# Where the loads of a group's gates and hidden values are issued in the V stage

## The reference, cut to what matters

```python
best, pos = lax.top_k(cand.reshape(tp, PEER_HEADS, PEER_TOPK * PEER_TOPK), PEER_TOPK)
ids = jnp.take_along_axis(cid.reshape(tp, PEER_HEADS, PEER_TOPK * PEER_TOPK), pos, axis=-1)
gates = jax.nn.softmax(best, axis=-1)
...
def block(args):
    xb, idb, gb = args
    h = jax.nn.gelu(jnp.einsum('td,thkd->thk', xb, u_table[idb]), approximate=False)
    w = (gb * h).astype(xb.dtype)
    return jnp.einsum('thk,thkd->td', w, v_table[idb]).astype(xb.dtype)
...
x = layer_norm(ALPHA * x + peer(x, peer_w_query, peer_sub_keys, peer_u, peer_v), ln2_g, ln2_b)
```

## Time and profile before

| what | value |
|---|---|
| median of 3 runs | 4085.16 us (4085.02 to 4093.54) |
| the profiled execution's own time | 4094.46 us |
| its span | 4092.7 us |
| mean granted TensorE clock of the span | 0.968 |
| PE busy / DVE busy / ACT busy / POOL busy | 96% / 64% / 26% / 36% |
| U stage ends, V stage's first matmul starts | 2845.6 us, 2853.4 us |
| last matmul of the V stage ends | 4049.4 us |

### The profile page before, as it was taken

The page is one execution under the profiler, slowest core; times in us unless marked ns, Lnnn a source line. Parts: engine busy times, 40 slices in busy tenths (PEclk is TensorE's granted clock), DMA queues, the critical chain, the costliest instruction groups (busy, mean ns, idle before and its releaser), DMA issues.

```text
span 4092.7 us, 70828 instructions
## 1 busy us (share of the span) xinstructions
PE 3908.7 (96%) x27864; PEld 3831.7 (94%) x27864; DVE 2617.1 (64%) x4474; ACT 1051.8 (26%) x914; POOL 1470.2 (36%) x497
## 2 busy tenths in 40 slices
PE   8999998796999999999999999999999999999996
PEld 7999998796999999999999999999999999999995
DVE  5776957656899299999972000001587787887867
ACT  3222322323222233333332222222222221222213
POOL 3232332344333333333334333434444344442311
PEclk9988988898999999999999999999999999999998
DMA  3221221221235656666666666665677778778752
GB/s 136 79 72 59 81 65 72 80 82 52 82 123 166 199 192 211 218 224 210 225 213 200 198 194 199 198 199 192 234 266 293 294 287 313 265 286 311 279 208 85
DMA packets 416196, 751.55 MB, mean 184 GB/s; under 512 B 19600, under 2 KB 343632, under 8 KB 355296
## 3 DMA queue, kind: packets, MB, share of 16 engines
q1 hardware_dynamic: 351936, 543.27, 39.4%
q0 software_dynamic: 22528, 134.30, 8.2%
q10 hardware_dynamic: 41632, 72.67, 5.0%
HBM read 677.60 MB, written 206.78 MB: 216 GB/s over the span
## 4 chain that ended last, share of the span: by engine, by line
PE 76%; DVE 14%; DMA 4%; issue 2%; ACT 2%; POOL 1%; SPq 1%; ACTq 0%; DVEq 0%; POOLq 0%
PE ps L534 52%; PE ps L778 19%; DMA wraw<-in_v_t 4%; DVE yb L1305 2%; PE ps L745 2%; DVE wl L1506 2%; PE ps L656 1%; PE ps L611 1%; PE ps L658 1%; ACT wh L837 1%; SPq L362 1%; DVE acc L1500 1%; DVE y_sp L1519 1%; DVE yfb L1314 0%; POOL wl L464 0%
## 5 line engine op out<-in xcount | busy, mean ns | idle before, releaser
L464 POOL TENSOR_TENSOR wl<-wraw,wh 128x2048 fp32r<-128x2048 f32 x202 | 961.0, 4758 | 1753.3 <-ACT wh L837 1753.3
L534 PE MATMUL ps<-xh,wh 128*128 128x272 f32 x5888 | 1241.3, 292 | 50.8 <-POOL xl L483 22.0
L534 PE MATMUL ps<-xh,wl 128*128 128x272 f32 x5888 | 1228.6, 290 | 0.0
L534 PE MATMUL ps<-xl,wh 128*128 128x272 f32 x5888 | 1225.2, 290 | 0.0
L534 PEld LDWEIGHTS ps<-xh,wh 128*128 128x128 f32 x5888 | 935.2, 191 | 63.9 <-issue 52.7
L534 PEld LDWEIGHTS ps<-xl,wh 128*128 128x128 f32 x5888 | 936.1, 191 | 0.0
L534 PEld LDWEIGHTS ps<-xh,wl 128*128 128x128 f32 x5888 | 930.5, 191 | 0.0
L837 ACT ACTIVATE wh<-wraw 128x2048 fp32r<-128x2048 f32 x328 | 628.5, 1916 | 1145.5 <-PE ps L778 732.8
L778 PE MATMUL ps<-Wh,wh 128*128 128x416 f32 x2048 | 721.9, 352 | 29.3 <-DVE wl L1506 21.2
L778 PE MATMUL ps<-Wh,wl 128*128 128x416 f32 x2048 | 724.8, 354 | 0.0
L778 PE MATMUL ps<-Wl,wh 128*128 128x416 f32 x2048 | 717.4, 350 | 0.0
(11 more groups left out here) (235 smaller groups left out, 2906.4 us busy)
## 6 DMA issues: line engine op xcount, KB each, us to landing
wraw<-in_u_t SPq DMA_DIRECT2D x128, 1024.0 KB, 5.0
v_rows<-in_v_t SPq DMA_DIRECT2D x256, 512.0 KB, 6.9
wraw<-in_v_t SPq DMA_DIRECT2D x128, 1024.0 KB, 5.1
wraw<-in_w_in SPq DMA_DIRECT2D x40, 1024.0 KB, 5.0
h_scratch<-hb ACTq DMA_DIRECT2D x64, 416.0 KB, 3.9
g_scratch<-gst ACTq DMA_DIRECT2D x13, 2048.0 KB, 7.7
gt<-g_scratch SPq DMA_DIRECT2D x16, 1664.0 KB, 14.1
hg<-h_scratch SPq DMA_DIRECT2D x16, 1664.0 KB, 20.5
```

What stands on the lines that cost most here:

```text
L464: nc.gpsimd.tensor_tensor(wl[:, u], wraw[:, u], f(wh[:, u]), ALU.subtract).then_inc(wlo, 1)
L534: ins = mat(out[:, h], w[:, u, k], m[:, k, halves[h]], start=(begin and k == ks[0] and w is wh and m is ah), stop=(end and k == ks[-1] and ...
```

## The change

`group_in` moves from SP's stream to ACT's, with the waits that guard it. On ACT the loads of group 0 stand behind the whole U stage: behind the last gelu, the last high part and the last stores of h. Those of group g+1 stand in group g's first iteration (m = 0), behind the high part of tile 8g+2. ACT's loop over pairs of tiles becomes a loop over groups with its 8 tiles written out. SP's stream keeps the weight tiles alone. No transfer, no computation and no semaphore count is otherwise changed.

```diff
-            for v in range(2):
-                sp.wait_ge(g_st[v], 16 * (NGC // 2 + 1))
-            for v in range(2):
-                sp.wait_ge(h_st[v], 32 * (EG // 4))
-            group_in(0)
             v_first()
-            sp.wait_ge(w_s, EG)
-            for v in range(2):
-                sp.wait_ge(h_st[v], 32 * (NKEY // 4))
-            group_in(1)
             v_pairs(0, EG // 4, EG // 2)
-            with sp.Fori(1, NG - 1) as g:
-                v_pairs(g, 0, EG // 4)
-                sp.wait_ge(w_s, g * EG + EG)
-                group_in(g + 1)
-                v_pairs(g, EG // 4, EG // 2)
-            with sp.Fori(NG - 1, NG) as g:
+            with sp.Fori(1, NG) as g:
                 v_pairs(g, 0, EG // 2)
...
             with C.loop(U_C, {h_out: 4}) as i:
                 u_four(i + (U_A + U_B))
...
+            def group_in(g):
+                for dst, src, q in ((gt[:].rearrange("p c e t -> p c (e t)"), gsrc, g_in),
+                                    (hg[:].rearrange("p (n u) t -> p n (u t)", u=2), hsrc, h_in)):
+                    s = src[g] if isinstance(g, int) else src[bass.ds(g, 1)].rearrange("o p n q -> (o p) n q")
+                    a.dma_start(dst, s).then_inc(q, 16)
+
+            for v in range(2):
+                a.wait_ge(g_st[v], 16 * (NGC // 2 + 1))
+            for v in range(2):
+                a.wait_ge(h_st[v], 32 * (EG // 4))
+            group_in(0)
             for e in range(EG):
                 a.wait_ge(wp_s, e + 1)
                 go(Wh[0][:, e], wt[e % 2][:], ACT.Copy).then_inc(wh_s, 1)
-            with a.Fori(0, (NG - 1) * EG // 2) as i:
-                for u in range(2):
-                    hi(i * 2 + (A_V + u + 2), u, i * 4 + (A_V + 2 * u + 2))
+            for v in range(2):
+                a.wait_ge(h_st[v], 32 * (NKEY // 4))
+            with a.Fori(0, NG - 1) as g:
+                for m in range(EG):
+                    hi(g * EG + (A_V + m + 2), m % 2, g * KT + (A_V + 2 * m + 2))
+                    if m == 0:
+                        a.wait_ge(w_s, g * EG + EG)
+                        group_in(g + 1)
```

More of the change, by code:

```diff
@@ L408, in _ @@
                              v_src[bass.ds(g, 1), m, d].rearrange("o j e c -> (o j) e c"), rows_in)
-            gsrc = g_dram.rearrange("c j (g e) t -> g j c (e t)", e=EG)
-            hsrc = h_dense.rearrange("(g n) p u t -> g p n (u t)", n=EG // 2)
             vs = v_t.rearrange("(g n u) p k c -> g n u p k c", u=2, n=EG // 2)
[L413 to L417, removed]
             def v_first():
@@ L1107, in _ @@
                 u_four(i + (U_A + U_B))
+            gsrc = g_dram.rearrange("c j (g e) t -> g j c (e t)", e=EG)
+            hsrc = h_dense.rearrange("(g n) p u t -> g p n (u t)", n=EG // 2)
+            def group_in(g):
[8 more added lines that the diff above has]
+            group_in(0)
             for e in range(EG):
```

## The result

The changed kernel has a median of 4115.87 us (4103.46 to 4132.46, 7 runs) beside 4090.31 us (4085.02 to 4094.42, 7 runs) of the kernel before; ratio 1.0067, interval 1.0046 to 1.0088. Two more jobs gave 1.0102 (1.0079 to 1.0124) and 1.0096 (1.0072 to 1.0121) for the same kernel. The forecast was 4081 us, within 4068 to 4104. Its profiled execution took 4125.55 us, 31.1 us more than the one before.

What follows compares the result with a forecast made beforehand. The V stage was taken as bound by TensorE at 9.06 us a tile, with 21.2 us of waits to save. +13.8 - 21.2 - 4 + 7 = -4.4 us gave a median of 4081 us, range 4068 to 4104.

Steps and rivals of the forecast that it cites:

- The start (+13.8): V stage's start: group 0's loads, late on ACT's queue, delay TensorE's first matmul; loss 13.8 us, bounds 11 and 22.5.
- The tile itself goes at the same pace: First V tile after the longer starting wait: same pace and no further clock cost, so nothing added to 13.8 us.
- the sum: Whole kernel against the profiled execution: +13.8 - 21.2 - 4 + 7 = -4.4 us.
- Tiles overtake the group (-21.2): Groups 2 to 15: tile 8g+4 no longer stands behind the group loads, taking off up to 21.2 us of TensorE's waits.
- E: In each group g of the V stage, the end of tile 8g, from which landing and due times are counted.
- Rival C: V tiles do not overtake and land as late as now; only SP's long issues go: +5, 4090 us; chance 0.12.
- hg late (+7): Groups 2 to 15: hg lands late in busy groups, 5 of 14 waiting 1 to 1.5 us, plus a little clock: +7 us.
- The byte sum: Window before hg is complete: 9.65 MB in 24.7 us puts hg at E + 26 to 27, lighter groups E + 23 to 24.
- The clock (-4): Two low-clock stretches behind TensorE's waits go with those waits; 5.1 us of lost work, of which 4 taken as gain.
- ACT's issue hides: Group loads issued on ACT: about 1 us for hg, even 5 us hidden by ACT's idle time; cost nothing.
- the groups' part: Groups' terms together, waits for tiles -21.2, clock -4 and late hg +7: -18 us.

Runs made afterwards that it cites:

- paced: The changed kernel with GpSimd clearing a 128x1024 tile after each of the 32 gathers of h, to issue them further apart; ratio 1.0046 to the kernel before.
- pool_late: The changed kernel with GpSimd starting its 32 gathers of h only when TensorE has finished V tile 1; ratio 1.0047 to the kernel before.
- early_2: Repeat of the kernel with group 0's loads on SP and later groups' loads on ACT, groups 2 to 15 one tile earlier than the change; 4062.61 us, ratio 0.9938.
- third: The changed kernel unaltered, run once more for a third profile; ratio 1.0096 to the kernel before.
- sp_first: The changed kernel with group 0's loads back on SP ahead of the first V tiles, groups 1 to 15 staying on ACT; ratio 0.9998 to the kernel before.
- act_first: The kernel before with group 0's loads alone moved to ACT behind the U stage, all other groups on SP; ratio 1.0082 to the kernel before.
- sp_late: The kernel before with group 0's loads on SP but held back until the last gelu of the U stage; ratio 1.0031 to the kernel before.
- late_act: The kernel before, loads early on SP, with ten extra copies on ACT that DVE waits for before W of group 0; ratio 1.0081 to the kernel before.
- early: First job with group 0's loads on SP and later groups' on ACT, groups 2 to 15 one tile earlier than the change; 4061.37 us, ratio 0.9949.

## Why the prediction was wrong, step by step

**The start (+13.8): right in mechanism and size.** Measured 14.4 us; hg had landed when DVE started at 2866.0, for 2865.2 forecast. That the longer wait would cost no further clock was right too in `paced` and `pool_late`, where nothing else disturbs the stage's start.

**The step that failed: "The tile itself goes at the same pace".** I concluded it from the clock alone, from a wait of 18.6 us earlier in the kernel. GpSimd issued no gathers behind that one. In the changed kernel its gathers of h go out 1.25 us apart while TensorE stands idle, and a slow stretch follows, 24.1 us in the profiled pair, where the prediction had nothing. The kernels with the wait alone (`pool_late`, `paced`) are at 1.0047 and 1.0046 and the changed kernel at 1.0067, 1.0102 and 1.0096, so an estimate across jobs gives the stretch 0.2 to 0.6%, 8 to 23 us. No rival had it. Without it the sum would have been +14.4 - 7.7, 7 us of loss in the profiled pair, inside the range.

**Tiles overtake the group (-21.2): right for the tiles.** ACT's waits for V tiles fell from 185.1 to 90.7 us but did not go. In nine groups tile 8g+4 kept ACT waiting until E + 18 to 20, later than my E + 17, still ahead of the E + 22.8 at which it is due; some 7 us of each such wait are ACT's usual idle time. Rival C is out. That the 21.2 us of TensorE's waits go with it was wrong: the late hg took their place, as the next step says. The Trainium skill has it that transfers of the three queues interleave on the same 16 DMA engines and that issuing from several of them saves only the sequencer's issue time (Trainium Kernel Development and Optimization, Key Constraints). By the second half the tiles would have stayed as late as they were; here the measurement decides against that, 90.7 us for 185.1; with the first half, turns between the queues, it agrees.

**hg late (+7): too low.** DVE waited for hg in each group: 0.9 to 5.4 us in groups 2 to 14, 33.3 us in all. These waits ended at E + 24.5 to 28.9, 26.4 in the mean, where I had 23 to 27 for the landing; I had taken 5 of 14 groups to wait. One group, timeline of DVE, with E = 3267.3:

```profile
3288.43 2.28 DVE L1503 TENSOR_TENSOR wl<-wraw,wh 128x2048 fp32r<-128x2048 f32 x1
3292.74 1.09 DVE L1484 TENSOR_TENSOR wt<-hg,gt 128x416 f32<-128x416 f32 x2 [2.02 <-DMA hg<-h_scratch]
```

The byte sum was sound within 2 us for these groups, and 7.4 us of TensorE's waits come from them. The other 6.1 us is the last group's, which I had not set apart: hg took ACT's queue 12.85 us to issue there and reached DVE 10.1 us late. Timeline of ACT and its queue:

```profile
3930.43 12.85 ACTq L1094 DMA_DIRECT2D hg<-h_scratch  x1
3943.48 1.91 ACT L815 ACTIVATE wh<-wraw 128x2048 fp32r<-128x2048 f32 x1 [11.89 <-PE ps L756]
```

The kernel before has the same long issue in the same group, 11.10 us, and I had put it down to what stood ahead of it on SP's queue. ACT's queue had only gt ahead of it, as in every group. The last group's issue is long in each of the twelve profiles with its load at this place, 9.9 to 11.1 us on SP and 11.4 to 15.6 on ACT; with the same loads one tile earlier (`early_2`) it took 1.60 us, while three others took 6 to 11. What sets the length is open. New waits are 13.5 us instead of 7, and up to 27.7 in `third`.

**The clock (-4): nothing.** The profile after has two dips behind waits in the groups, as before (length, busy, clock, DMA share, GB/s), and so the lost work is the same:

```profile
3970.00:3978.00 8.00, 5.66 (x18) 0.57 0.57 216
4002.00:4009.00 7.00, 4.85 (x25) 0.76 0.26 82
```

0.43 x 8 + 0.24 x 7 = 5.1 us, the sum I had for the kernel before.

The first dip lies behind the last group's wait of 6.1 us. The second lies behind a wait of 2.1 us that the kernel before has too, without a dip behind it (`PE ps <- DVEq`, L798 here and L820 there).

**ACT's issue hides: right.** 0.7 to 5.4 us in 15 groups, behind it only the high part of tile 8g+3; the last delayed that part by 4.7 us, without a wait of TensorE of its own.

Together the groups' part was to be -18 us and was -7.7 us in the profiled pair, +10.5 in `third` against the same profile of before, and -0.8 us (-6.5 to +4.5) in the runs of `sp_first`. Why it differs so from run to run is open.

## What stays open

That an idle TensorE and unpaused gathers are both needed is shown: take away either and the stretch goes. That they are enough is not: `act_first`'s profile has both and hardly a pause. Whether the gathers' pace or their number before the first V matmul counts (11 and 12 with a slow stretch, 0 to 7 without, 12 beside a busy TensorE) was not tested. How gathers of 128 elements of 4 bytes hold TensorE up is not. The late release of ACT and DVE would fit a path for instructions or semaphore updates that both use, but no run separates the two. How long the wait must be is open as well: 17.3 us (`sp_late`) were too few, 20.6 us (`late_act`) enough, yet the two also differ in when the gathers begin.

## What to carry to other kernels

A load that opens a stage belongs in the stream that gets there first, for a queue's issue point is the place in its engine's instruction stream. When loads change queues, add up the bytes of the window and ask when the moved one lands, then move it until it lands with room: here one tile of 9 us turned no change (`sp_first`) into 0.5 to 0.6% faster. Before a gain in waits is believed, read it in a second profile: the same kernel had 13.5, 18.3 and 27.7 us of them. A wait that is only priced by its length may cost more behind it: look at what other engines do during it.

## What the runs showed of the hardware that was not expected

- The slow stretch: 20 matmuls of 416 columns in 26 us at a granted clock of 0.60, every operand ready, after 22.3 us without a matmul and beside indirect gathers 1.25 us apart. Four profiles have it, 16 to 40 matmuls in the 26 us; it is gone with gathers 2.2 us apart or held back, or with TensorE kept busy.
- Of the six runs of `early` one, the profiled one, took 21507 us, the others 4056 to 4069. It was slow in every stage alike, at a granted clock of 1.0. Groups of TensorE instructions there (busy, mean ns of one); the kernel before has 292 and 352 ns:

```profile
L520 PE MATMUL ps<-xh,wh 128*128 128x272 f32 x5888 | 5272.6, 1084 | 24.9 <-POOL xl L469 13.7 <-DVE ext L1292 9.6 <-ACT picksT L1066 1.6
L764 PE MATMUL ps<-Wh,wh 128*128 128x416 f32 x2048 | 2962.2, 1446 | 7.9 <-DVE Wl L1532 7.9
```

  It did not come again in six runs of the same program, and whether it has to do with the slow stretch is open.
- Queues take turns by packets, not bytes: the 1 KB packets of gt stood against 8 KB ones at like counts, and a byte sum over the window still gave hg's landing within 2 us, the last group's excepted.
